# Moving the on-chip tensors of a fused transformer kernel to other start addresses

## The reference, cut to what matters

```python
D_MODEL = 1024; SEQ = 512; D_FF = 2816
# first block
u = rmsnorm(h, norm_mix_pre);  (...) = split(u @ w_in)
ya = gdn_mixer(...)            # gated delta rule, 4 heads of 128
yb = nsa_mixer(...)            # sparse attention, 8 heads of 64
mixed = (g_a * (ya @ w_a2d) + g_b * (yb @ w_b2d)) @ w_o
h = h + rmsnorm(mixed, norm_mix_post)
f = causal_dwconv(rmsnorm(h, norm_ffn_pre) @ w_up, conv_ffn) + conv_ffn_b
f = (gelu(f_gate) * f_val) @ w_down;  h = h + rmsnorm(f, norm_ffn_post)
e = (p @ w_ple) * sigmoid(h @ w_ple_gate);  h = h + rmsnorm(e, norm_ple_post)
# second block
proj = rms_norm(h, mix_norm_g) @ w_in_2
attn_out = moba_attention(...);  conv_out = conformer_conv(...)   # 31 taps
h = h + concatenate([attn_out, conv_out]) @ w_out_2
u = rms_norm(h, ffn_norm_g)
h = h + (silu(u @ w_gate_2) * (u @ w_up_2)) @ w_down_2
return rms_norm(h, final_norm_g)
```

## Time and profile before

| | |
|---|---|
| median of three runs | 1797.57 us |
| the profiled execution itself | 1797.66 us |
| its span, first to last instruction | 1795.8 us |
| PE busy | 1661.6 us, 93% |
| PEld busy | 1365.9 us, 76% |
| DVE busy | 942.1 us, 52% |
| ACT busy | 644.4 us, 36% |
| POOL busy | 143.9 us, 8% |
| mean granted TensorE clock | 0.948 |
| HBM read | 128.94 MB, 73 GB/s |

### The profile page before, as it was taken

One profiled execution on the slowest core, in us unless ns is written; L12 is line 12 of the kernel. 1 busy time (PEld: TensorE's weight loads), 2 busy tenths in 40 slices (PEclk: granted clock), 3 DMA queues, 4 the chain that ended last, 5 costly groups with the idle time before them and its releaser, 6 DMA issues. The chain is left out here.

```text
span 1795.8 us, 20947 instructions
## 1 busy us (share of the span) xinstructions
PE 1661.6 (93%) x8022; PEld 1365.9 (76%) x8022; DVE 942.1 (52%) x1282; ACT 644.4 (36%) x898; POOL 143.9 (8%) x108
## 2 busy tenths in 40 slices
PE   7996999999999979999999988886899999999997
PEld 6886987878788858888878756664577788887885
DVE  4635346267433366777732255799854444444233
ACT  4542432045322234444422234243364434442211
POOL 0003401000000020000000000157310000000000
PEclk9988999899899989999999978998888999999998
DMA  4210004000132302322222212221002222221221
GB/s 166 95 59 1 1 6 190 19 18 1 36 105 93 109 32 96 114 93 93 79 97 85 100 59 85 92 74 47 24 1 91 74 94 95 101 106 66 80 96 63
DMA packets 22846, 131.91 MB, mean 73 GB/s; under 512 B 2604, under 2 KB 3116, under 8 KB 12924
## 3 DMA queue, kind: packets, MB, share of 16 engines
q1 hardware_dynamic: 20672, 122.69, 19.5%
q0 software_dynamic: 816, 6.15, 0.9%
q10 hardware_dynamic: 1296, 2.21, 0.3%
HBM read 128.94 MB, written 2.10 MB: 73 GB/s over the span
## 5 line engine op out<-in xcount | busy, mean ns | idle before, releaser
L305 PE MATMUL ps<-AH,whi 128*128 128x512 f32 x1280 | 514.3, 402 | 60.2 <-DVE wlo L292 22.8
L306 PE MATMUL ps<-AL,whi 128*128 128x512 f32 x1280 | 507.5, 396 | 0.0
L307 PE MATMUL ps<-AH,wlo 128*128 128x512 f32 x1280 | 506.7, 396 | 0.0
L292 DVE TENSOR_TENSOR wlo<-raw,whi 128x2048 fp32r<-128x2048 f32 (+4 forms) x126 | 255.5, 2028 | 279.7 <-ACT whi L285 279.3
L305 PEld LDWEIGHTS ps<-AH,whi 128*128 128x128 f32 x1280 | 245.6, 192 | 127.7 <-DVE wlo L292 26.1
L307 PEld LDWEIGHTS ps<-AH,wlo 128*128 128x128 f32 x1280 | 245.8, 192 | 52.6
L306 PEld LDWEIGHTS ps<-AL,whi 128*128 128x128 f32 x1280 | 246.3, 192 | 50.1
L285 ACT ACTIVATE whi<-raw 128x2048 fp32r<-128x2048 f32 (+4 forms) x126 | 210.6, 1671 | 202.5 <-PE ps L307 202.5
L305 PE MATMUL ps<-HH,whi 128*128 128x512 f32 x352 | 140.4, 399 | 5.3 <-issue 5.3
L306 PE MATMUL ps<-HL,whi 128*128 128x512 f32 x352 | 140.0, 398 | 0.0
L307 PE MATMUL ps<-HH,wlo 128*128 128x512 f32 x352 | 140.0, 398 | 0.0
(11 more groups left out here) (347 smaller groups left out, 2134.8 us busy)
## 6 DMA issues: line engine op xcount, KB each, us to landing
raw<-wstream SPq DMA_DIRECT2D x74, 1024.0 KB, 4.8
raw<-wstream SPq DMA_DIRECT2D x32, 704.0 KB, 3.9
raw<-wstream SPq DMA_DIRECT2D x16, 768.0 KB, 4.0
raw<-wstream SPq DMA_DIRECT2D x8, 640.0 KB, 3.7
hT<-xT SPq DMA_DIRECT2D x4, 512.0 KB, 6.9
W1k<-w1k_d POOLq DMA_DIRECT2D x1, 2048.0 KB, 9.7
W1v<-w1v_d POOLq DMA_DIRECT2D x1, 2048.0 KB, 16.4
raw<-wstream SPq DMA_DIRECT2D x2, 512.0 KB, 3.4
```

Of the source, the lines that this page charges most:

```text
L292: nc.vector.tensor_tensor(WL[b][:, 0:n], RAW[b][:, 0:n], WH[b][:, 0:n].bitcast(F32), ALU.subtract).then_inc(w_lo_done, 1)
L305: nc.tensor.matmul(out_, WH[b][:, w], xh[:, k, :], start=start and k == 0, stop=False)
L306: nc.tensor.matmul(out_, WH[b][:, w], xl[:, k, :], start=False, stop=False)
L307: last = nc.tensor.matmul(out_, WL[b][:, w], xh[:, k, :], start=False, stop=stop and k == n - 1)
```

## The change

Only the layout changes, and with it one DMA's destination. `cols` (475 columns) gets four columns more and goes ahead of `hT`; the four are the old tensor `RC`. They take 1,916 bytes, so `hT` then starts at 18,432, which is 9 times 2048. `ones` and `ident` go behind `YX`. In the first block's scope the tensors that TensorE streams come first, the small ones (`SG`, `NG_T`, `MB`) behind them with an unused tensor of 512 bytes. In the second block's scope `MB2` goes behind, and `CU` ahead of `UG`, whose rows have 542 values.

```diff
+HOME = 2048
...
+        cols = sb("cols", [P, NCOLS + T])
+        RC = cols[:, NCOLS:NCOLS + T]
         hT = sb("hT", [P, DC, S])
         AH = sb("AH", [P, DC, S], F32R)
         AL = sb("AL", [P, DC, S], F32R)
         RAW = [sb(f"raw{b}", [P, BLK * P]) for b in range(2)]
         WH = [sb(f"whi{b}", [P, BLK * P], F32R) for b in range(2)]
         WL = [sb(f"wlo{b}", [P, BLK * P], F32R) for b in range(2)]
-        cols = sb("cols", [P, NCOLS])
-        ones = sb("ones", [P, P])
-        ident = sb("ident", [P, P])
         RR = sb("RR", [P, S])
         SQ = sb("SQ", [P, 2, S])
         TMP = sb("TMP", [P, 2, S])
         YX = sb("YX", [P, S])
         SF = YX
-        RC = sb("RC", [P, T])
+        ones = sb("ones", [P, P])
+        ident = sb("ident", [P, P])
...
         blk1 = ExitStack()
-        SG = sb("SG", [P, T, 32], F32, blk1)
-        NG_T = sb("NG_T", [P, P], F32, blk1)
-        MB = sb("MB", [P, 2, P], BF16, blk1)
...
         YAH = sb("YAH", [P, 4, S], F32R, blk1)
         YAL = sb("YAL", [P, 4, S], F32R, blk1)
+        SG = sb("SG", [P, T, 32], F32, blk1)
+        NG_T = sb("NG_T", [P, P], F32, blk1)
+        MB = sb("MB", [P, 2, P], BF16, blk1)
+        sb("filler1", [P, (HOME - 3 * 4 * P) // 4], F32, blk1)
...
         with ExitStack() as x:
-            MB2 = sb("MB2", [P, P], F32, x)
             QT2 = sb("QT2", [P, 4, S], F32, x)
...
+            CU = sb("CU", [P, CC, S], F32, x)
             UG = sb("UG", [P, CC, S + CT - 1], F32, x)
-            CU = sb("CU", [P, CC, S], F32, x)
+            MB2 = sb("MB2", [P, P], F32, x)
...
-            act.dma_start(cols[:, :], cols_d).then_inc(cols_landed, 16)
+            act.dma_start(cols[:, 0:NCOLS], cols_d).then_inc(cols_landed, 16)
```

## The result

Six runs of the changed kernel took 1783.09 to 1788.31 us, median 1783.83; six of the kernel before 1793.26 to 1798.12, median 1797.39. The ratio is 0.9942, with a 95% interval from 0.9923 to 0.9960. A later comparison on another chip gave 1782.96 against 1797.64 us, ratio 0.9916 [0.9903, 0.9929]. The forecast was 1786.4 us. The profiled execution took 1785.23 us with a span of 1783.2.

A forecast was written before the change was run, and what follows sets the result against it. TensorE's streaming pace was taken to bound up, mix and down, VectorE the convolution. From 1797.66 us, 11.5 us of shorter pace less 0.2 us for stage boundaries gave 1786.4 us, forecast 1783 to 1790, wider range 1774 to 1799.

The forecast's parts named there:

- The bound: TensorE's pace is the time in up, mix and down; ScalarE waits 202.5 us for it; VectorE bounds only the convolution.
- Part 1, the size: Slow streams in mix, ple and down: 1488 matmuls reach 226.7 ns, 7.5 ns less each, 11.2 us; 11.5 with small terms.
- Part 1, the cause: Streams starting 32 bytes past a multiple of 512 are slow, those at multiples of 128 fast: the stream's start sets the pace.
- Part 2: `AH`, `AL` and weights move from rest 128 to 0: 3840 matmuls, taken as 0; bounds 51 us gain, 28.8 us loss.
- The gate matmuls: 24 matmuls streaming `AH` against weights starting at rest 544 take 232.9 ns each; 24 x 6.2 = 0.15 us gain.
- Part 3: VectorE operations, convolution taps, DMAs, filler and `RC` inside `cols`: taps change by 0.5 us at most, taken as 0.
- The sum: Whole execution: 11.5 us saved, less 0.2 us for stage boundaries, from 1797.66 to 1786.4 us.
- The second: Every stream loses its surplus and reaches 215.8 ns, gaining 27.4 and 40.3 us, to 1730 us; chance 0.13.
- The third: Place above byte 130,000, not the start, makes streams slow; paces stay and the time is 1797.6 us; chance 0.12.
- The fourth: `AH`/`AL` and weights on the same round address collide in up, up2 and mix; 1826 or 1815 us; chance 0.09.

The follow-up runs named there:

- hidden_far: The changed kernel with 160 bytes ahead of `HH`, so `HH` and `HL` alone have the old distance from the weights; median 1792.79 us, ratio to the kernel before 0.9972.
- only_high: The kernel before with `RC` inside `cols`: upper tensors on multiples of 512, `hT`, `AH`, `AL` and weights left at 128; median 1792.60 us, ratio 0.9988.
- bench_starts: Computation left out, TensorE alone, 40 matmuls per pair of starts; stream at 32 took 9.33 us with weights at 0, 9.11 us with weights at 32.
- bench_distances: Computation left out, weights at a multiple of 2048, 40 matmuls with the stream at each distance; 226.7 ns at 0, 256, 512, 1024 and 1536.
- one_shift: The kernel before with one unused tensor of 96 bytes ahead of `SG` and nothing else; median 1783.01 us, ratio to the kernel before 0.9935.
- weights_odd: The changed kernel with 32 bytes ahead of `WH`: `AH`, `AL` stay at multiples of 2048, weights begin at 32; 1807.31 us, ratio to the kernel before 1.0080.

## Why the prediction was right, and what it had wrong

- **The bound.** Right. A shorter pace in mix and down came out as time, and the wait of ScalarE for TensorE fell only from 202.5 to 197.7 us.
- **Part 1, the size.** Right: `HH` and `GHI` went from 234.3 to 226.7 ns over the whole trace, as the sum's 1488 x 7.5 = 11.2 us takes for all. The small ones gave a little less (`YAH` and `YBH` 233.5 to 226.7, `PH` 233.2 to 226.8). hidden_far gives back the part of `HH` at 9.8 us for 7.9 of the sum.
- **Part 1, the cause.** Wrong. The step that failed is the sentence that the pace follows the rest of the stream's start. All weights of the kernel before had the rest 128, so a stream's start and its distance from the weights could not be told apart in that trace, and I took the simpler of the two. The forecast came out because the change sets both to zero, and in this it was lucky. For half the change (only_high) the same reasoning promised 11 us and the runs showed no gain that can be told from none.
- **Part 2.** It was costed at 0 with the right observation, that the distance for `AH` is 0 before and after, and it does bring nothing to `AH`. But in this change the gain needs it: by it the weights move to the round address at which the upper tensors then lie. Costing the two parts one by one hid that.
- **The gate matmuls.** Forecast 0.15 us by their weights' start. Right in sign and small: with their start at 0 they take 5.55 us against 5.59, here 95.86 to 101.41 in the timeline. In bench_starts the 40 matmuls with weights of 32 columns take 9.27 us, 232 ns, even at distance 0. So the distance was at most 1.6 of their 6.2 ns.
- **Part 3.** Right, see the unchanged VectorE rows. The taps of the convolution still take 1198 ns on average: 746 where GpSimd is idle and 1650 where it works beside them for more than half of the tap, before and after. The idle gap of 4.43 us between up2 and down2 is there again with the same length.
- **The sum.** 11.5 us forecast, 12.4 between the two profiled executions, 13.6 and 14.7 us between medians. By the span's mean granted clock, 0.948 before and 0.949 after, the halved clock took (1 - 0.948) x 1795.8 = 93 us and (1 - 0.949) x 1783.2 = 91; that the surplus of 1 to 3 us is this clock is likely and not shown.
- **The rivals.** The second (all surplus gone) falls by bench_distances: no distance is below 226.7. The third (place) falls by the pairs above byte 150,000, and by one_shift, where the tensors stay high and have 226.7 ns. The fourth had the right pair of operands with the wrong sign: a common start of stream and weights is the good case, not the collision.

## What to carry to other kernels

Give fp32r streams of 512 columns and their weights (blocks 512 bytes apart) the same start modulo 256 bytes; a filler of 96 bytes did here what the new layout did, some 14 us of 1797. Read TensorE's pace from start to start, for each pair of tensors, and compare tensors streamed against the same weights. When two explanations always go together in a trace, the gain may be forecast rightly and still be lost by the next edit: move one operand alone before writing down the rule.

## What the runs showed that I had not expected

- The pace of fp32r matmuls of 512 columns by distance modulo 256 at the full clock: 226.7 ns at 0, 229 at 64, 231 to 233 at the others tried, 234.4 at 160, and 238 with a stream 4 bytes off.
- The surplus is one of fp32r at the full clock: bf16 has 216 ns and plain fp32 429 for twice 213.3. At the halved clock fp32r has 426 to 427 ns wherever it streams without a break: `AH` at distance 0, `HH` at 160 in the kernel before, `AH` at 224 in weights_odd.
- With 256 columns distance 32 was the quicker one (117.8 against 120.0 ns); with 384, 320 and 192 columns both took the same, 173.3, 146.7 and 111.7 ns.
- After a break or a change of starts the pace of 226.7 ns often comes only after up to eight matmuls at 224 to 241 (bench_starts).
